# A sample tile's high and low parts as one 128-column stationary operand in the projections of a two-layer encoder step

## What is computed

```python
def trunk(x, ...):
    for layer in range(DEPTH):                      # 2
        if layer % 2 == 0:
            y = ab_mixer(x, ...)                    # u, va, q, k, v = split(x @ ab_w_in);  heads;  ... @ ab_w_out
        else:
            y = c_mixer(x, ...)                     # q, k, v, qi, ki, wi = split(x @ c_w_in);  top-k attention;  ... @ c_w_out
        x = layer_norm(ALPHA * x + y, ln1_g[layer], ln1_b[layer])
        x = layer_norm(ALPHA * x + sq_relu_mlp(x, ff_w1[layer], ff_w2[layer]), ln2_g[layer], ln2_b[layer])

y_prompt, ... = trunk(x_prompt, pos_p, ...)         # 1024 rows
y_sample, ... = trunk(x_sample, pos_s, caches, ...) # 64 rows
```

## Time and profile before

| | us |
|---|---|
| median of 3 runs | 2787.55 |
| lowest and highest | 2786.24, 2788.78 |
| the profiled execution, its span | 2790.9 |
| in it: PE busy | 2646.1 (95%) |
| PEld | 2323.7 (83%) |
| DVE | 1546.9 (55%) |
| ACT | 922.8 (33%) |
| POOL | 175.6 (6%) |

### The profile page before, as it was taken

How to read it: one execution, slowest core, us unless ns; L and a number is a source line. 1 busy time by engine, 2 the same in 40 slices (tenths; PEclk the granted TensorE clock), 3 DMA queues, 4 the chain that set the end, 5 groups by cost and what they waited for, 6 DMA issues and landing times. The chain is left out here.

```text
span 2790.9 us, 36346 instructions
## 1 busy us (share of the span) xinstructions
PE 2646.1 (95%) x14198; PEld 2323.7 (83%) x14198; DVE 1546.9 (55%) x2793; ACT 922.8 (33%) x1762; POOL 175.6 (6%) x168
## 2 busy tenths in 40 slices
PE   7999999999999999979969988899999999999996
PEld 6778789989899999868757777887898999999895
DVE  2445363444444444566889799963634444444535
ACT  3207343323222222322044555562532222223231
POOL 0300040000000000300020000000400000000003
PEclk9999999999999999989965898899999999999998
DMA  4110311101010101131100000003110101011011
GB/s 136 46 41 1 115 49 45 61 30 60 30 60 30 60 30 45 61 94 31 44 8 1 1 1 1 1 30 121 59 46 31 60 30 59 31 42 48 30 46 65
DMA packets 81279, 124.25 MB, mean 45 GB/s; under 512 B 6224, under 2 KB 54736, under 8 KB 81168
## 3 DMA queue, kind: packets, MB, share of 16 engines
q1 hardware_dynamic: 81168, 122.74, 13.4%
HBM read 110.98 MB, written 11.75 MB: 44 GB/s over the span
## 5 line engine op out<-in xcount | busy, mean ns | idle before, releaser
L1213 PE MATMUL psum<-xt_hi,layer_w_hi 128*128 128x384 f32 (+1 forms) x1536 | 505.5, 329 | 3.2 <-DVE xt_lo L847 3.2
L1215 PE MATMUL psum<-xt_hi,layer_w_lo 128*128 128x384 f32 (+1 forms) x1536 | 505.0, 329 | 0.0
L1214 PE MATMUL psum<-xt_lo,layer_w_hi 128*128 128x384 f32 (+1 forms) x1536 | 504.9, 329 | 0.0
L1128 DVE TENSOR_TENSOR act<-psum,act 128x512 f32<-128x512 f32 x540 | 366.2, 689 | 233.6 <-PE psum L1251 230.7
L1249 PE MATMUL psum<-layer_w_hi,layer_h_split 128*128 128x512 f32 x1024 | 400.0, 391 | 2.8 <-DVE layer_h_split L1116 1.6
L1250 PE MATMUL psum<-layer_w_lo,layer_h_split 128*128 128x512 f32 x1024 | 399.3, 390 | 0.0
L1251 PE MATMUL psum<-layer_w_hi,layer_h_split 128*128 128x512 f32 x1024 | 399.1, 390 | 0.0
L1116 DVE TENSOR_TENSOR layer_h_split<-layer_h_raw,layer_h_split 128x384 fp32r<-128x384 f32 (+1 forms) x192 | 98.4, 512 | 352.8 <-ACT layer_h_split L1029 352.8
L1213 PEld LDWEIGHTS psum<-xt_hi,layer_w_hi 128*128 128x128 f32 x1536 | 288.3, 188 | 4.7 <-DVE xt_lo L847 3.5
L1214 PEld LDWEIGHTS psum<-xt_lo,layer_w_hi 128*128 128x128 f32 x1536 | 288.4, 188 | 1.3
L1215 PEld LDWEIGHTS psum<-xt_hi,layer_w_lo 128*128 128x128 f32 x1536 | 288.4, 188 | 0.0
(11 more groups left out here) (215 smaller groups left out, 4067.5 us busy)
## 6 DMA issues: line engine op xcount, KB each, us to landing
layer_w_raw<-in_ff_w SPq DMA_DIRECT2D x64, 1024.0 KB, 6.3
ab_in_w_raw<-in_ab_w_in SPq DMA_DIRECT2D x12, 512.0 KB, 4.5
c_in_w_raw<-in_c_w_in SPq DMA_DIRECT2D x12, 512.0 KB, 3.9
ab_in_xt_raw<-in_xT SPq DMA_DIRECT2D x8, 512.0 KB, 4.2
layer_resid<-in_x SPq DMA_DIRECT2D x16, 256.0 KB, 2.8
x_scratch<-act SPq DMA_DIRECT2D x8, 512.0 KB, 2.6
layer_resid<-x_scratch SPq DMA_DIRECT2D x16, 256.0 KB, 2.7
out_y_prompt<-act SPq DMA_DIRECT2D x8, 512.0 KB, 2.6
```

The source lines that it names most:

```text
L1128: dve.tensor_tensor(acc, banks[4 + g % 4][0:r], acc, ALU.add).then_inc(y_read, 1)
L1213: pe.matmul(out, w1_hi[:, k, w], xt_hi[:, k, a:b], start=(k == 0), stop=False)
L1214: pe.matmul(out, w1_hi[:, k, w], xt_lo[:, k, a:b], start=False, stop=False)
L1215: mm = pe.matmul(out, w1_lo[:, k, w], xt_hi[:, k, a:b], start=False, stop=(k == KT - 1))
```

## The change

- `xt_hi` becomes 64 columns wider. The sample tile's low part is no longer put into `xt_lo` but behind its high part, so that both stand side by side as 128 columns. The transposes inside the layers (`x1`) keep the old place.
- The sample product has 16 matmuls instead of 24: for each of the 8 channel groups one of the 128 stacked columns with w_hi, which puts x_hi w_hi into the bank's rows 0 to 63 and x_lo w_hi into rows 64 to 127, and one of the 64 high columns with w_lo into rows 0 to 63. `used` and `done` are counted at the same places.
- DVE folds the two row halves. In `ab_in` and `c_in` the new `join_halves` copies rows 64 to 127 into a buffer in SBUF (`total`), waits for that, adds rows 0 to 63, counts `joined` and waits for it; the rotary positions, the GELU (on ACT, which waits for `joined` there) and the copies of the sample then read `total`. In the layers a second add follows the residual's, behind a new semaphore, `high_added`.
- In `ab_in` `total` takes the place of one x buffer that is done with, and the buffer of the rotary positions becomes single, with a wait to suit.
- The scratch size for DMAs that GpSimd would generate is set to 4096.

```diff
--- before.py
+++ after.py
...
-        xt_hi = split.take("xt_hi", [P, KT, TOK], F32R)
+        xt_hi = split.take("xt_hi", [P, KT, TOK + DEC], F32R)
         xt_lo = split.take("xt_lo", [P, KT, TOK], F32R)
+        xt = xt_hi, xt_lo
...
-    def product(self, pe, out, t, j, xt_hi, xt_lo):
+    def product(self, pe, out, t, j, xt):
 
         a, b = tok(t)
         w = self.chunks[j][1]
+        xt_hi, xt_lo = xt
         for q in range(4):
             n = 4 * j + q
             if t == 0:
@@ -285,9 +287,17 @@
             for k in range(QUARTER):
                 kk = QUARTER * q + k
                 first, last = kk == 0, kk == KT - 1
-                pe.matmul(out[0:b - a, 0:w], xt_hi[:, kk, a:b], self.hi[:, s, k, 0:w], start=first, stop=False)
-                pe.matmul(out[0:b - a, 0:w], xt_hi[:, kk, a:b], self.lo[:, s, k, 0:w], start=False, stop=False)
-                mm = pe.matmul(out[0:b - a, 0:w], xt_lo[:, kk, a:b], self.hi[:, s, k, 0:w], start=False, stop=last)
+                if t == SAMPLE:
+                    stacked = lambda: pe.matmul(out[:, 0:w], xt_hi[:, kk, SEQ:TOK + DEC], self.hi[:, s, k, 0:w], start=first, stop=last)
+                    if not last:
+                        stacked()
+                    mm = pe.matmul(out[0:b - a, 0:w], xt_hi[:, kk, a:b], self.lo[:, s, k, 0:w], start=False, stop=False)
+                    if last:
+                        mm = stacked()
+                else:
+                    pe.matmul(out[0:b - a, 0:w], xt_hi[:, kk, a:b], self.hi[:, s, k, 0:w], start=first, stop=False)
+                    pe.matmul(out[0:b - a, 0:w], xt_hi[:, kk, a:b], self.lo[:, s, k, 0:w], start=False, stop=False)
+                    mm = pe.matmul(out[0:b - a, 0:w], xt_lo[:, kk, a:b], self.hi[:, s, k, 0:w], start=False, stop=last)
...
+def low_part(xt, t):
+
+
+    a, b = tok(t)
+    return xt[1][:, :, a:b] if t < SAMPLE else xt[0][:, :, TOK:TOK + DEC]
+
+
+def join_halves(dve, link, bank, total, joined, n):
+
+
+    w = total.shape[1]
+    link(dve.tensor_copy(total, bank[DEC:2 * DEC, 0:w]))
+    dve.tensor_tensor(total, bank[0:DEC, 0:w], total, ALU.add).then_inc(joined, 1)
+    dve.wait_ge(joined, n)
...
-        tmp = room.take("rope_tmp", [P, 2, 2, 8, HD], F32)
+        tmp = room.take("rope_tmp", [P, 2, 8, HD], F32)
+        total = xr[:, 1, 0:COLS // P].rearrange("p k q -> p (k q)")
+        joined = c(nc.semaphore(tag + "sample_joined"))
...
                         g, r = j * NT + t, rows(t)
-                        act.wait_ge(done, g + 1)
+                        if t == SAMPLE:
+                            act.wait_ge(joined, j + 1)
+                        else:
+                            act.wait_ge(done, g + 1)
                         out = A[0:r, t, 0:A_WIDTH] if j == 0 else va[0:r, t]
-                        act.activation(out, banks[g % 8][0:r], ACT.Gelu_apprx_tanh).then_inc(evac_act, 1)
+                        src = total[0:r] if t == SAMPLE else banks[g % 8][0:r]
+                        act.activation(out, src, ACT.Gelu_apprx_tanh).then_inc(evac_act, 1)
...
-                    turn = tmp[0:r, g % 2]
+                    turn = tmp[0:r]
                     if t == NT - 1:
                         for n in st.next_pieces(j):
                             st.split_lo(dve, n)
+                    bank = banks[g % 8][0:r]
+                    if t == SAMPLE:
+                        dve.wait_ge(done, g + 1)
+                        if j in (1, 2):
+                            dve.wait_ge(evac_act, j * NT)
+                        join_halves(dve, link, banks[g % 8], total[0:r, 0:chunks[j][1]], joined, j + 1)
+                        bank = total[0:r]
...
-                        if t >= 2:
-                            dve.wait_ge(evac_dve, t - 1)
-                        src = banks[g % 8][0:r].rearrange("p (h d) -> p h d", d=HD)
+                        if t >= 1:
+                            dve.wait_ge(evac_dve, t)
+                        src = bank.rearrange("p (h d) -> p h d", d=HD)
...
-                        dve.wait_ge(evac_dve, g - 1 - 2 * NT)
-                        src = banks[g % 8][0:r, 0:P].rearrange("p (h d) -> p h d", d=HD)
+                        dve.wait_ge(evac_dve, g - 2 * NT)
+                        src = bank[:, 0:P].rearrange("p (h d) -> p h d", d=HD)
...
-                        dve.tensor_copy(vb[0:r, slot], banks[g % 8][0:r, P:2 * P]).then_inc(evac_dve, 1)
+                        dve.tensor_copy(vb[0:r, slot], bank[:, P:2 * P]).then_inc(evac_dve, 1)
...
+    def low_part(self, n):
+        t, h = divmod(n, 2)
+        a, b = tok(t)
+        if t == SAMPLE and self.stacked:
+            return self.hi[:, 4 * h:4 * h + 4, TOK:TOK + DEC]
+        return self.lo[:, 4 * h:4 * h + 4, a:b]
...
+                 "x1": Turn(nc, c, tag, "x1", A, xt, ident, lambda n: banks[bank_number(("x1", n))], stacked=False)}
...
-                dve.scalar_tensor_tensor(out=A[0:r, t, j * COLS:(j + 1) * COLS], in0=xr[0:r, g % RESID], scalar=ALPHA,
-                                         in1=banks[bank_number(("out", j, t))][0:r], op0=ALU.mult, op1=ALU.add).then_inc(freed, 1)
+                out, bank = A[0:r, t, j * COLS:(j + 1) * COLS], banks[bank_number(("out", j, t))]
+                summed = dve.scalar_tensor_tensor(out=out, in0=xr[0:r, g % RESID], scalar=ALPHA, in1=bank[0:r],
+                                                  op0=ALU.mult, op1=ALU.add)
+                if t == SAMPLE:
+                    summed.then_inc(high_added, 1)
+                    dve.wait_ge(high_added, j + 1)
+                    summed = dve.tensor_tensor(out, bank[DEC:2 * DEC], out, ALU.add)
+                summed.then_inc(freed, 1)
...
+        total = room.take("sample_total", [P, COLS], F32)
+        joined = c(nc.semaphore(tag + "sample_joined"))
...
                     dve.wait_ge(done, g + 1)
                     if g >= 1:
                         dve.wait_ge(read, g)
+                    if t == SAMPLE:
+                        join_halves(dve, link, banks[g % 4], total[0:r, 0:chunks[j][1]], joined, j + 1)
+                        bank = total[0:r]
...
+    nc = bacc.Bacc("TRN2", target_bir_lowering=False, num_devices=1, dynamic_dma_scratch_size=4096)
```

More of the change, by code:

```diff
@@ L538, in _ @@
                             pe.wait_ge(evac_dve, before + 1 - 2 * NT)
-                    st.product(pe, banks[g % 8], t, j, xt_hi, xt_lo)
+                    st.product(pe, banks[g % 8], t, j, xt)
 def block_ab_mixer(nc, aps, room, A, va, kb, vb, ident, early, ps):
@@ L817, with __init__ @@
 class Turn:
-    def __init__(self, nc, c, tag, name, A, xt_hi, xt_lo, ident, bank_of):
-        self.A, self.hi, self.lo, self.ident, self.bank_of = A, xt_hi, xt_lo, ident, bank_of
+    def __init__(self, nc, c, tag, name, A, xt, ident, bank_of, stacked=True):
+        self.A, self.ident, self.bank_of = A, ident, bank_of
+        (self.hi, self.lo), self.stacked = xt, stacked
         self.turned = c(nc.semaphore(tag + f"{name}_turned"))
@@ L831, in transpose, with high_part @@
         mm.then_inc(self.turned, 1)
-    def view(self, x, n):
+    def high_part(self, n):
         t, h = divmod(n, 2)
         a, b = tok(t)
-        return x[:, 4 * h:4 * h + 4, a:b]
+        return self.hi[:, 4 * h:4 * h + 4, a:b]
+    def low_part(self, n):
[4 more added lines that the diff above has]
+        return self.lo[:, 4 * h:4 * h + 4, a:b]
     def bank(self, n):
@@ L842, in high, with block_layer @@
         act.wait_ge(self.turned, n + 1)
-        act.copy(self.view(self.hi, n), self.bank(n)).then_inc(self.hi_made, 1)
+        act.copy(self.high_part(n), self.bank(n)).then_inc(self.hi_made, 1)
     def low(self, dve, n, freed):
         dve.wait_ge(self.hi_made, n + 1)
-        dve.tensor_tensor(self.view(self.lo, n), self.bank(n), self.view(self.hi, n), ALU.subtract).then_inc(freed, 1)
-def block_layer(nc, aps, room, w_room, layer, resid, w_out, A, xt_hi, xt_lo, ident, mhalf, stored, early, ps, next_early=None):
+        dve.tensor_tensor(self.low_part(n), self.bank(n), self.high_part(n), ALU.subtract).then_inc(freed, 1)
+def block_layer(nc, aps, room, w_room, layer, resid, w_out, A, xt, ident, mhalf, stored, early, ps, next_early=None):
     w1 = aps["ff_w1"][layer].rearrange("(k p) (n f) -> p k n f", p=P, f=FC)
@@ L914, in block_layer @@
         freed, scaled = sem("banks_freed"), sem("alpha_scaled")
-        turns = {"mix": Turn(nc, c, tag, "mix", A, xt_hi, xt_lo, ident, lambda n: banks[bank_number(("mix", n))]),
-                 "x1": Turn(nc, c, tag, "x1", A, xt_hi, xt_lo, ident, lambda n: banks[bank_number(("x1", n))])}
+        high_added = sem("resid_high_rows_added")
+        turns = {"mix": Turn(nc, c, tag, "mix", A, xt, ident, lambda n: banks[bank_number(("mix", n))]),
+                 "x1": Turn(nc, c, tag, "x1", A, xt, ident, lambda n: banks[bank_number(("x1", n))], stacked=False)}
         w1_in, w2_in = sem("w1_arrived"), sem("w2_arrived")
@@ L923, in block_layer @@
```

(8 more changed lines are left out.)

14 lines of the change are left out of this document (7 added, 7 removed).

## The result

The median went from 2788.16 to 2804.34 us in the first four runs of each, a ratio of 1.0054 (95% interval 1.004 to 1.0067); twelve more runs gave 1.0032 (1.0017 to 1.0048). By these ratios the change makes the kernel some 9 to 15 us slower; the medians themselves lie 16 and, in the twelve more runs, 13 us apart. The forecast was 2786.3, and the measured time lies above the range. The profiled execution's span is 2802.7 against 2790.9.

A forecast was written before the change was run, and what follows sets the result against it. The prediction took PE's waits on DVE weight splits at chunk changes as the bound. Its terms, -0.98 (ab_in), -0.82 (layers) and +0.59 (c_in), sum to -1.21 us: 2786.3 us, range 2782.0 to 2790.5.

The forecast's parts named there:

- What bounds the kernel: At seven of eight chunk changes PE waits for a DVE weight split, so shorter products mostly become waiting.
- layer 0's chunk: Layer 0's chunk change: the split chain hangs on the first quarter's end, six matmuls becoming four, -0.46 us.
- the MLP product that waits for L847: Layer's end: w2 split, L847 and then PE move by 0 to +0.12 us, taken as +0.05.
- The folds: In c_in, DVE copy and add of 0.68 us each plus waits, 1.42; third change +1.30 after a shorter V copy.
- rival 4: Sample products: wider weight loads stall PE, none gets shorter, only folds remain, 3.7 us; 2791.2 us; chance 0.04.
- `ab_in`'s first change: First chunk change in ab_in: same split chain as layer 0, -0.46 us.
- The waits' price: Layer 0's chunk change: of 1.84 us saved per product, PE waits 1.38; no term for a slower clock afterwards.
- rival 1: PE cools during c_in's third-change wait of 4.1 us, clock falls once: 1.6 us lost, 2787.9 us; chance 0.11.
- `ab_in`: chunk changes and fold: ab_in's three chunk changes, -0.46, -0.12 and -0.40, and its end fold, 0: sum -0.98 us.
- the two layers: chunk changes and second add: Each layer -0.46 at its chunk change and +0.05 at its end, so -0.41; both -0.82 us.
- `c_in`: chunk changes and folds: c_in: -0.29 at the first change, +1.30 at the third, -0.42 at the end; sum +0.59 us.
- Rival 3: Half-clock stretch in the sparse attention changes length: 2782 or 2793 us; chance 0.04 shorter, 0.06 longer.

The follow-up runs named there:

- e2: Kernel after with one more 64-column matmul by zeros per channel group in sample products (24 matmuls), folds kept: 2792.89 us, ratio 1.0017 to the kernel before.
- e3: Kernel before with extra VectorE subtractions ahead of the last L847 of each output projection, two in layer 0, four in layer 1: 2792.44 us, ratio 1.0005.
- e8: Kernel after with c_in's sample tile back at 24 matmuls and no fold there: 2793.46 us, ratio 1.0011 to the kernel before.
- e9 to e11: Kernel after with one, two and four added VectorE adds of 512 columns at c_in's end: 2796.59, 2796.49 and 2800.42 us.
- e7: Kernel after with third weight-piece buffer; second chunk of each output projection keeps 24 matmuls, no second add: 2766.21 us, ratio 0.9916 to the kernel before.
- e4: Kernel after with a third buffer for arriving weight pieces: 2774.13 us, ratio 0.9938 to the kernel before.
- e6: Kernel before with a third buffer for arriving weight pieces, 24 matmuls and no fold: 2781.46 us, ratio 0.997 to the kernel before.
- e5: Kernel after run once more, unchanged, twelve runs: 2802.59 us, ratio 1.0032 to the kernel before.

## Why the prediction was wrong

**What bounds the kernel: right.** The chunk changes hang on the split chain, and the shorter product turned into waiting. A sample product of layer 0 ends 3.7 us after it begins, and PE then waits 1.45 us. The table above shows layer 0's chunk at -0.51 us (forecast -0.46), and the stretch from there to the MLP product that waits for L847 has not changed at all (425.17 - 362.07 = 426.65 - 363.55 = 63.10; forecast +0.05). That product is not the MLP's first: products over the earlier tiles' columns run from 413.35 on in before (413.01 after), between the last transposes, and only the group that takes in the last tile waits.

**The folds: right.** In `c_in`, DVE:

```profile
1315.08 0.69 DVE L399 COPY c_in_sample_total<-psum 64x512 f32<-64x512 f32 x1
1315.81 0.68 DVE L400 TENSOR_TENSOR c_in_sample_total<-psum,c_in_sample_total 64x512 f32<-64x512 f32 x1
...
1317.73 0.28 DVE L1644 COPY c_v<-c_in_sample_total 64x256 f32<-64x256 f32 x1
...
1356.99 2.35 DVE L270 TENSOR_TENSOR c_in_w_lo<-c_in_w_raw,c_in_w_hi 128x1024 fp32r<-128x1024 f32 x2
```

Copy and add take 0.69 and 0.68, the V copy from SBUF 0.28 in place of 0.41: the 0.13 that the prediction worked out from the Trainium skill ("VectorE: DVE Perf Modes", Why PSUM operands drop a tier), and the trace agrees with it. The splits at 1352.42 came to 1356.99, 4.57 later, of which 3.10 had come by the change before (1309.90 to 1313.00): 1.47 for the fold, and PE resumed 1.53 later in the same terms, where +1.30 was forecast. In e2, with 24 matmuls, all folds together cost about 4 us; rival 4 had 3.7.

**`ab_in`'s first change: mis-sized.** Forecast -0.46; the chunk took 49.77 us against 49.63. The first of the two loads that it hangs on was issued as much earlier as forecast (67.79 against 67.51, in a stage that ran 0.74 late by then), but landed after 4.2 us in place of 3.6. The second is issued 1.1 us behind it in place of 1.3; whether that is the reason was not tried.

**The waits' price: the step that failed.** The prediction wrote "PE waits the other 1.38 us" and took that for free: no term of its sum prices how fast PE runs after a wait. It held the fall of the clock possible at one place, `c_in`'s third change, as rival 1 with a chance of 0.11 and 1.6 us. The place was right (2.7 us), but it is five places in the trace of after, and waits of 1.8 us do it, not only of 4. The argument against it, that PE is busy without a pause before the wait, was wrong. In after PE was busy without a pause, at full clock, up to the wait of 1.80 us at 123.72, and the clock fell all the same (windows view):

```profile
76.00:121.80 45.80, 45.80 (x203) 37.19 (x201) 16.30 (x36) 12.54 (x19) 19.49 (x23) 1.00 0.12 39
```

How far the trace of after lags behind that of before can be read at every sample product and every resumption of PE. The steps of that lag, added up:

| us | forecast | measured |
|---|---|---|
| `ab_in`: chunk changes and fold | -0.98 | -0.66 |
| the two layers: chunk changes and second add | -0.82 | -1.24 |
| `c_in`: chunk changes and folds | +0.59 | +0.75 |
| clock behind five waits | 0 | +10.76 |
| ahead of each stage's first sample product, and the rest | 0 | -0.11 |
| outside the sparse attention | -1.21 | +9.50 |

So the moved chains came to what the prediction had, -1.2, by some luck: its blocks are off by +0.3, -0.4 and +0.2. The miss outside the sparse attention is the clock behind the waits, 10.8 us that the sum had at nothing. The row before the last stands where the change does nothing yet: +0.7 in `ab_in`, +0.2 in layer 0, +0.9 in layer 1, and -2.0 in `c_in`, where before has a wait of 1.84 us with a clock of 0.50 behind it (1211.73 to 1215.14) and after a wait of 0.69 without. The rule that the prediction cited from the Trainium skill ("TensorE: Matmul & The Clock Gate", What's actually happening), that the throttled state is the default, stood on the right side; e3 shows what it costs here, 1.3 to 1.6 us behind one wait.

**Rival 3, the sparse attention**, differs by some 10 us from trace to trace, where the prediction took up to 5.5, and not in this kernel alone: single runs of the kernel before spread from 2784 to 2801 us. In the kernel after 11 of 16 runs were over 2800, with `c_in` plain (e8) none of 12. Why it is long more often after this change stays open: e9 to e11 don't settle it, and e7, with the stacked `c_in`, has the short one. The 9.5 us outside it are shown; what it adds on top, up to 6 us by the ratios, isn't explained.

## What to carry to other kernels

Where an engine's work ends in a wait, cutting that work buys little, and on TensorE it can cost: here two microseconds of idle time between busy stretches brought, at some places, 3 us and more at half the clock. First take away what the wait hangs on (here one more buffer of 4 KB per partition), then shorten the work: the same stacked operand that lost 9.5 us outside the sparse attention then gained 13 there (by the medians of e4 and e6, 7). Before a change to a chunk's last tile, read the granted clock behind each wait as well as the wait's length.

## What the runs showed of the hardware

After a wait of TensorE of 1.6 to 3.7 us between stretches of full work, the granted clock of the next 5 us was 1.00 at some places and 0.50 to 0.71 at others, with no fixed length that parts them: 1.59 us (e7, layer 0) and 1.69 (e2, layer 1) were enough once, 2.60 us (e2, `c_in`) was not, and at the end of layer 1 the kernel after had 0.50 after 2.20 us in its first trace and 1.00 after 2.19 in its second (e5). The loss was 1.3 to 2.7 us each, beyond the wait itself. And a stage with instructions unchanged, the sparse attention, takes 465 to 468 or 474 to 478 us from one trace to the next; PE is busy for 401 us of it in e8 and 416.5 in the kernel after, so here too the granted clock differs; why it does was not found. The windows view of e8, clock 0.81, from the stage's first row to its last:

```profile
1412.60:1880.06 467.46, 401.03 (x2622) 350.48 (x2623) 421.60 (x894) 264.43 (x625) 38.45 (x24) 0.81 0.02 5
```

And of after, clock 0.78:

```profile
1415.75:1892.20 476.45, 416.51 (x2622) 367.24 (x2623) 422.27 (x894) 263.99 (x625) 38.43 (x24) 0.78 0.02 5
```
